# A two-layer retention and convolution decoder step on one Trainium2 core: moving conv-state and ple-input DMAs to the queue of the weight loads, reordering two steps at the ple end, and merging two transposes

## The reference, cut to what matters

```
z = rms_norm(x) @ w_in                      # 7168 columns: q, k, v, g_r, a, b, g_c
q, k = rope(q), rope(k); o, S = retention(q, k, v, S0)   # 8 heads x 128
ret = group_norm(o) * silu(g_r)
u = a * sigmoid(b)
full = concat([conv_state, u]); c = causal depthwise conv, width 31
c = silu(layer_norm(c)) @ w_pw2 * silu(g_c)
h = x + rms_norm(concat([ret, c]) @ w_out)
e = rms_norm(p[i] @ w_ple)                  # p: 256 wide, per layer
x = h + sigmoid(h @ w_gate) * e
```

## Time and profile before

| | us |
|---|---|
| median of 3 runs | 1210.65 (1210.05 to 1211.07) |
| the profiled execution's own time | 1209.43 |
| its span, first to last instruction | 1207.6 |
| PE busy in the span | 1190.3 (99%) |
| DVE busy | 921.4 (76%) |
| ACT busy | 605.7 (50%) |
| POOL busy | 87.6 (7%) |

### The profile page before, as it was taken

One profiled execution on the slowest core, in us unless ns is written; L12 is line 12 of the kernel. 1 busy time (PEld: TensorE's weight loads), 2 busy tenths in 40 slices (PEclk: granted clock), 3 DMA queues, 4 the chain that ended last, 5 costly groups with the idle time before them and its releaser, 6 DMA issues.

```text
span 1207.6 us, 25290 instructions
## 1 busy us (share of the span) xinstructions
PE 1190.3 (99%) x9804; PEld 1185.7 (98%) x9804; DVE 921.4 (76%) x1465; ACT 605.7 (50%) x917; POOL 87.6 (7%) x104
## 2 busy tenths in 40 slices
PE   6999999999999999999999999999999999999998
PEld 6999999999999999999999999999999999999998
DVE  6799799999986643588869979999999764346863
ACT  7333565555556444545444435555555554455341
POOL 0000000000010011201110000000000100121000
PEclk9999999999999999999999999999999999999999
DMA  8455755545555654424546565555555445543462
GB/s 306 173 209 197 215 204 187 192 177 194 192 180 173 238 181 174 175 91 155 209 175 216 202 205 200 203 184 185 186 207 203 162 174 216 196 148 138 144 212 100
DMA packets 43466, 225.80 MB, mean 187 GB/s; under 512 B 6401, under 2 KB 13057, under 8 KB 19585
## 3 DMA queue, kind: packets, MB, share of 16 engines
q1 hardware_dynamic: 29520, 200.14, 46.4%
q10 hardware_dynamic: 13872, 24.65, 6.3%
HBM read 210.97 MB, written 13.81 MB: 186 GB/s over the span
## 4 chain that ended last, share of the span: by engine, by line
PE 88%; DVE 5%; issue 3%; DMA 2%; ACT 2%; ACTq 1%; DVEq 0%; SPq 0%
PE accum_all L475 26%; PE accum_all L476 26%; PE accum_all L477 26%; PE ps L541 2%; DMA raw<-w_in 1%; PE accum_all L566 1%; DVE wlo L1088 1%; PE accum_all L567 1%; PE accum_all L568 1%; DVE tmp L1164 1%; ACT whi L719 1%; DVE c_buf L1164 1%; DMA pre<-w_in 1%; PE ps L491 1%; PE ps L516 1%
## 5 line engine op out<-in xcount | busy, mean ns | idle before, releaser
L475 PE MATMUL accum_all<-a_hi,whi 128*128 128x264 f32 x2048 | 585.2, 286 | 2.3 <-DVE wlo L1341 2.3
L476 PE MATMUL accum_all<-a_lo,whi 128*128 128x264 f32 x2048 | 580.3, 283 | 0.0
L477 PE MATMUL accum_all<-a_hi,wlo 128*128 128x264 f32 x2048 | 580.1, 283 | 0.0
L1088 DVE TENSOR_TENSOR wlo<-raw,whi 128x2048 fp32r<-128x2048 f32 x182 | 421.5, 2317 | 182.9 <-ACT whi L719 182.8
L719 ACT ACTIVATE whi<-raw 128x2048 fp32r<-128x2048 f32 x182 | 347.5, 1912 | 158.7 <-DMA raw<-w_in 85.7
L475 PEld LDWEIGHTS accum_all<-a_hi,whi 128*128 128x128 f32 x2048 | 385.8, 188 | 3.2 <-issue 2.5
L476 PEld LDWEIGHTS accum_all<-a_lo,whi 128*128 128x128 f32 x2048 | 386.1, 189 | 0.8
L477 PEld LDWEIGHTS accum_all<-a_hi,wlo 128*128 128x128 f32 x2048 | 384.1, 188 | 0.0
L475 PE MATMUL accum_all<-b_hi,whi 128*128 128x264 f32 x672 | 191.0, 284 | 0.0
L476 PE MATMUL accum_all<-b_lo,whi 128*128 128x264 f32 x672 | 190.4, 283 | 0.0
L477 PE MATMUL accum_all<-b_hi,wlo 128*128 128x264 f32 x672 | 190.3, 283 | 0.0
(11 more groups left out here) (213 smaller groups left out, 1260.8 us busy)
## 6 DMA issues: line engine op xcount, KB each, us to landing
raw<-w_in SPq DMA_DIRECT2D x108, 1024.0 KB, 4.8
raw<-w_out SPq DMA_DIRECT2D x32, 1024.0 KB, 4.8
raw<-w_gate SPq DMA_DIRECT2D x32, 1024.0 KB, 4.8
s_new<-s_ret ACTq DMA_DIRECT2D x16, 512.0 KB, 3.6
ss_out<-s_new ACTq DMA_DIRECT2D x16, 512.0 KB, 2.6
raw<-w_pw SPq DMA_DIRECT2D x8, 1024.0 KB, 4.8
x<-x_t SPq DMA_DIRECT2D x4, 528.0 KB, 7.7
raw<-w_in SPq DMA_DIRECT2D x8, 256.0 KB, 8.0
```

The source lines that it names most:

```text
L475: pe.matmul(accum[bank][:, 0:R], w_hi[:, w:w + P], hi, start=k == 0, stop=False)
L476: pe.matmul(accum[bank][:, 0:R], w_hi[:, w:w + P], lo, start=False, stop=False)
L477: mm = pe.matmul(accum[bank][:, 0:R], w_lo[:, w:w + P], hi, start=False, stop=k == k_tiles - 1)
L1088: v.tensor_tensor(wlo[:, slot, :], raw[:, side, :], whi[:, slot, :].bitcast(F32), ALU.subtract).then_inc(s.lo_ready, 1)
```

## The change

Four edits.

1. `scp_out`, `scs_out` and `p_in` are issued by SP and not by ACT. `p_in` comes after the load of slab 15. The loads of slabs 16 to 19 follow, then the wait for `ust_ready` and `convstate_in`, then `scp_out` and `scs_out`, and then the loads from slab 20 on.
2. ACT: `e_out(7)` stands ahead of `h_hi(1)`.
3. DVE: `add_m(2)` stands ahead of `h_lo(1)`.
4. The two transposes of 32 columns in `ret_scores` are one of 64 columns. ACT reads the second block from partitions 32 to 63.

```diff
@@ SP
-            with sp.Fori(0, HEADS) as h:
+            if l:
+                sp.wait_ge(s.pin_ready, l)
+            sp.dma_start(p_in[:, :, :], p_t[l, :, :, :]).then_inc(s.p_in, 16)
+            for j in range(4):
+                load(l, S_H + j, j, w_in, P * (in_row + HEADS * j))
+
+            sp.wait_ge(s.ust_ready, CT * (l + 1))
+            sp.wait_ge(s.convstate_in, 16 * (l + 1))
+            sp.dma_start(scp_out[l, :, :, :], u_buf[:, :, SEQ:SEQ + PAD]).then_inc(s.scp_out, 16)
+            sp.dma_start(scs_out[P * l:P * l + P, :].rearrange("p (c k b) -> p c k b", c=CT, k=PAD),
+                         ust[:, :, 1:TAPS, :]).then_inc(s.scs_out, 16)
+            with sp.Fori(1, HEADS) as h:
@@ PE, ret_scores
-            pe.transpose(ps_s1[0:32, 0:P], cols[:, 0:32], ident)
-            pe.transpose(ps_s1[0:32, P:2 * P], cols[:, 32:64], ident)
+            pe.transpose(ps_s1[0:64, 0:P], cols[:, 0:64], ident)
@@ ACT, ret_rows
-                block_of_b = nc.scalar.activation(vbd[0:32, b, :], ps_s1[0:32, P:2 * P], ACT.Copy,
-                                                  scale=cst[0:32, K_MASK + b:K_MASK + b + 1])
+                block_of_b = nc.scalar.activation(vbd[0:32, b, :], ps_s1[32:64, 0:P], ACT.Copy,
+                                                  scale=cst[32:64, K_MASK + b:K_MASK + b + 1])
@@ ACT, before head 0
-            act.wait_ge(s.ust_ready, CT * (l + 1))
-            act.wait_ge(s.convstate_in, 16 * (l + 1))
-            act.dma_start(scp_out[l, :, :, :], u_buf[:, :, SEQ:SEQ + PAD]).then_inc(s.scp_out, 16)
-            act.dma_start(scs_out[P * l:P * l + P, :].rearrange("p (c k b) -> p c k b", c=CT, k=PAD),
-                          ust[:, :, 1:TAPS, :]).then_inc(s.scs_out, 16)
-
-            if l:
-                act.wait_ge(s.pin_ready, l)
-            act.dma_start(p_in[:, :, :], p_t[l, :, :, :]).then_inc(s.p_in, 16)
             head(l, 0, False, False)
@@ ACT, end of the layer
             e_out(6)
+            e_out(7)
             h_hi(1)
-            e_out(7)
@@ DVE, end of the layer
                 scale_m(g)
+                if g == 2:
+
+                    add_m(g)
                 if g:
                     h_lo(g - 1)
-                add_m(g)
+                if g != 2:
+                    add_m(g)
```

## The result

| | before | changed |
|---|---|---|
| median, us | 1210.35 (1207.95 to 1211.54, 6 runs) | 1216.56 (1214.76 to 1218.58, 6 runs) |
| ratio, 95% interval | | 1.0059 (1.0047 to 1.0070) |
| profiled execution, its span, us | 1209.43, 1207.6 | 1217.38, 1215.6 |

A forecast was written before the change was run, and what follows sets the result against it. PE, busy 99% of the span, bounds the kernel; only its work or waits count. 5.2 + 5.1 - 1.5 - 0.4 = +8.4 us on 1210.65 gives 1219.0 us, range 1210.0 to 1225.0.

The forecast's parts named there:

- Slab 20 behind the outputs: Loads on SP: slab 20 lands behind both outputs, so its copy starts 5.2 us later in layer 0, 5.6 in layer 1.
- ACT's 5.3 us: Layer 0: time ACT gets back from three DMAs; can't reach DVE, as slab 20 lands at 123.9 at best, 0.4 us earlier.
- the two layers' terms: Losses around head 0 from slab 20 coming later: +5.2 us in layer 0 and +5.1 us in layer 1.
- PE in layer 0: Around head 0: new 2.9 us wait before tile 20, 3.5 us for stack_cols instead of 1.15; layer 0 +5.2 us.
- Everything as before, 5.2 us later: Layer 0, after the wait for stack_cols: PE goes on as before the change, only 5.2 us later.
- the clock falls: Rival: PE's clock falls in the new waits near head 0, +1 to +2 us per layer, 1220 to 1223 us; chance 0.1.
- the granted clock is 1.00 in every window I read: Evidence given against the rival of a falling PE clock: no window read in the old profile showed a lower clock.
- Layer 1: Around head 0: slab 20's copy 5.6 us later, s_new at 753.1 where PE was at 748.02: +5.1 us.
- the outputs' 7.0 us: DMA time of scp_out and scs_out ahead of slab 20, from busy shares: 10.6 - 2.85 - 0.7 = 7.0 us, both layers.
- The transposes: ret_scores, one transpose for two: 0.11 us saved for each of 14, -1.5 us; head 0's two vanish in a wait.
- The ple end: End of each layer's ple part: new wait of some 0.25 us for one of 0.49, -0.2 us per layer, -0.4 us.
- the third issue's 3.94 us: Layer 0, before head 0: the time for which the third DMA alone holds ACT, ahead of slab 20's copy.

The follow-up runs named there:

- the wait alone: Changed kernel, but ACT issues scp_out and scs_out again; SP keeps its wait before slab 20, and p_in: 1207.78 us against 1209.21 before the change.

## Why the prediction was right, and where its sizes were off

It said 1219.0 us, slower; it is 1216.56 us, in the range. By its own steps:

**Slab 20 behind the outputs: right.** Predicted: copies 11 to 13 us after `ust_ready`, waiting for raw. They are 12.05 us after the start of the last sample copy in layer 0 (11.8 behind its end) and a little short, 10.6, in layer 1. The step that ACT's 5.3 us can't reach DVE even with an empty queue was right too: with the wait alone the copy comes at 7.3 us, for 6.8 before. The other 4.8 us are the outputs ahead of the load, 1.4 by their issue and 3.4 by the ring. Edit 1 alone costs 9.4 us, where the two layers' terms were 10.3.

**PE in layer 0: right.** Tile 20's new wait was to be 2.9 us and is 2.90; `stack_cols` 3.5 and is 2.99. `ret_samples` starts 6.03 us later (154.54 to 160.57). Of that, 1.08 us are older than the change's first effect: the last sample copy starts at 117.49 before and at 118.57 after (the last section has more on this). Left are +4.95 for +5.2.

**"Everything as before, 5.2 us later": not quite.** The slow clock kept PE back for about 1.6 us behind `stack_cols`, so the wait for `pmat` vanished and that for `s_new` shrank. DVE's chain, not PE, set the time until 160.5: the fall cost nothing here. This is half of the rival "the clock falls": it did fall, in one layer, but its +1 to +2 us did not come. The rival had a wait behind it take up 1.7 us, and here the fall was no longer than that. With edit 1 alone it also fell in layer 1, for over 6 us, and there it cost some 0.9 us. So the rival was right as a mechanism, and a chance of 0.1 for it was low: what went wrong is the step "the granted clock is 1.00 in every window I read" as evidence against, since the kernel before has no wait of this length in its fast stretch. That the number held in spite of it is in part luck: in layer 0 the fall happened to be short enough.

**Layer 1: mis-sized.** +5.1 predicted, +3.5 measured from the last sample copy to `ret_samples` (the copy 10.60 for 6.48 us after the sample copy, +4.1 for +5.6). The term that failed is the outputs' 7.0 us, taken from busy shares for both layers: by the landings it is 11.8 - 4.8 = 7.0 us in layer 0 and 10.4 - 4.8 = 5.6 us in layer 1. With edit 1 alone layer 1 was 12.0 behind the issue (717.27 to 729.29). The term is no constant, and one value for two places gave a sum of some 1.5 us too much in this execution.

**The transposes: right.** Two heads of the changed kernel, the starts of `ret_samples` at 188.73 and 216.82, are 28.09 us apart, where it was 28.20 (182.78 to 210.98): -0.11 per head, -1.5 in all. **The ple end: right.** The waits for `e_buf` are gone, and the new one stands at the second group of steps, 0.25 us over the pace; net -0.2 us per layer. Together -1.9 predicted, 2.0 us measured with edit 1 undone. By its steps the change then makes 4.95 + 3.5 - 1.9 = +6.6 us, where the medians say +6.2.

**What the prediction didn't see** is the gain inside edit 1. It had the third issue's 3.94 us in hand, and rightly said that they can't reach DVE with slab 20 behind the outputs. It didn't ask what the edit would give with two loads ahead of the wait: 6.5 us instead of a loss of 6.2 (with edits 2 to 4 in both).

## What to carry to other kernels

Here a wait for something made late, on the queue that feeds the bottleneck, cost 4.4 us of a load's time, and two outputs of 1024 small pieces each ahead of the load another 4.8. So put the loads whose buffers are already free first, then the wait and the outputs. Before moving a DMA off a busy engine, look at which of its issues is long; here it was one of three, and moving that one alone won most of what there was. A load's landing time beside small writes on the other ring (6.7 us here) and behind them on its own (10.1) are two different numbers.

## What the runs showed of the hardware that was not expected

**The clock falls in short pauses.** The kernel before has a granted clock of 1.00 in every window; only its first matmuls, 0.22 us apart, were slow. In the profiled executions of the changed kernel and of the experiments, PE had twelve waits of 2.77 to 3.05 us in stretches where it had run fast, five near the start and seven around head 0. Behind eleven of them the granted clock went to 0.50 for 3 to 7 us; the exception is the 2.90 us before tile 20 in the changed kernel. Behind waits of 2.3 us and less it never did. The Trainium skill ("TensorE: Matmul & The Clock Gate", the clock gate) says that idle gaps between bursts of matmuls can send it back; the windows agree.

**The start of the program varies.** PE's second wait, whose code the change doesn't touch, was 1.3 to 2.3 us in five profiled executions and 2.8 to 3.0 us in five. This is the changed kernel behind the long one:

```profile
24.00:26.00 2.00, 1.60 (x8) 0.62 1.03 434
26.00:28.00 2.00, 2.00 (x11) 0.52 0.72 299
```

The last sample copy of layer 0 came at 116.3 to 117.5 in the first five (the kernel before among them) and at 118.6 to 118.8 in the others. That is up to 2.6 us between executions whose first 87 us are the same program, and the next 30 but for the place of `p_in`; it is as much as the 0.2% that a single run can't tell from no change. The clock fell behind that wait in the second five and in none of the first. The extra wait and the matmuls at half speed behind it add up to something of this size; no run took either away, so the cause isn't shown. A single profile's span has to be corrected for it before two kernels are compared.

**Small writes.** The time that two small-piece writes hold up a load differed by up to 1.7 us between layers and kernels with the same list on SP, and it didn't divide by bytes. On ACT, the issue of `p_in` behind those 2048 pieces held the engine for 3.5 to 3.9 us, where the two ahead took 0.6 to 0.7 us each. This is no rule for every third issue: on SP, the load of slab 20 behind the same two outputs was issued in 0.36 us (the row at 120.52), and `p_in` with nothing small ahead of it in 0.34. What makes the difference is not shown.
